# First block of a two-block transformer step: the recurrence's outputs with exchanged operands, and transfers inside SBUF in place of turns

## The reference, cut to what matters

```python
bu = einsum('bsgh,gph->bsgp', u, b_bar)          # 32 groups, 16 inputs, 64 complex states each
states = associative_scan(a_r * a_l, a_r * b_l + b_r) over the tokens
y = einsum('bsgp,ghp->bsgh', states, c_mat).real + d_skip * u
y = gelu(y.reshape(bsz, seq, 512))
y = y * sigmoid(y @ w_glu + b_glu)
mixed = concat([rmsnorm(y), rmsnorm(chunked_attention(q, k, v, rel_bias))])
```

## Time and profile before

| | us |
|---|---|
| median of 3 executions | 2977.44 (2976.95 to 2977.65) |
| span of the profiled execution, first to last instruction | 2975.0 |
| TensorE busy, of the span | 2961.7 |
| VectorE busy | 2261.4 |
| ScalarE busy | 1467.9 |
| the stage of the change | about 120 to 180 |

### The profile page before, as it was taken

How to read it: one execution, slowest core, us unless ns; L and a number is a source line. 1 busy time by engine, 2 the same in 40 slices (tenths; PEclk the granted TensorE clock), 3 DMA queues, 4 the chain that set the end, 5 groups by cost and what they waited for, 6 DMA issues and landing times.

```text
span 2975.0 us, 48001 instructions
## 1 busy us (share of the span) xinstructions
PE 2961.7 (100%) x18781; PEld 2655.5 (89%) x18781; DVE 2261.4 (76%) x2787; ACT 1467.9 (49%) x2155; POOL 58.1 (2%) x148
## 2 busy tenths in 40 slices
PE   9999999999999999999999999999999999999999
PEld 8779999888889999878899998888999878899998
DVE  7978888576759887566598875658888567588984
ACT  4476555454345555444455553325555354355554
POOL 6100000000000000000000000000000000000000
PEclk9999999999999999999999999999999999999999
DMA  6122332342133332311333333223333222133322
GB/s 189 49 72 92 101 125 93 111 137 71 56 101 99 99 105 100 94 64 56 105 101 99 99 107 105 87 68 115 102 100 106 92 85 66 62 114 99 106 99 78
DMA packets 256759, 283.30 MB, mean 95 GB/s; under 512 B 11938, under 2 KB 229216, under 8 KB 256616
## 3 DMA queue, kind: packets, MB, share of 16 engines
q1 hardware_dynamic: 256504, 281.28, 29.1%
q10 hardware_dynamic: 112, 0.02, 0.0%
HBM read 279.16 MB, written 4.73 MB: 95 GB/s over the span
## 4 chain that ended last, share of the span: by engine, by line
PE 89%; DVE 6%; ACT 2%; issue 1%; POOL 1%; DMA 1%; DVEq 0%; SPq 0%; ACTq 0%; POOLq 0%
PE ps L2946 39%; PE ps L2571 13%; PE ps L2573 13%; PE ps L2572 13%; PE ps L3303 1%; PE ps L3304 1%; PE ps L3305 1%; PE ps L3210 1%; PE ps L3270 1%; PE ps L3249 1%; PE ps L3289 1%; PE ps L3291 1%; PE ps L3290 1%; PE ps L3159 1%; PE ps L3140 0%
## 5 line engine op out<-in xcount | busy, mean ns | idle before, releaser
L840 ACT ACTIVATE whi<-raw 128x2048 fp32r<-128x2048 f32 (+2 forms) x144 | 246.6, 1712 | 467.8 <-PE ps L2573 386.7
L1519 DVE TENSOR_TENSOR wlo<-raw,whi 128x2048 fp32r<-128x2048 f32 (+2 forms) x144 | 293.6, 2039 | 219.5 <-ACT whi L840 219.2
L2946 PE MATMUL ps<-th,wh 128*128 128x256 f32 x1600 | 453.7, 284 | 0.6 <-DVE wl L1608 0.5
L2946 PE MATMUL ps<-tl,wh 128*128 128x256 f32 x1600 | 452.7, 283 | 0.0
L2946 PE MATMUL ps<-th,wl 128*128 128x256 f32 x1600 | 452.7, 283 | 0.0
L2571 PE MATMUL ps<-hh,whi 128*128 128x512 f32 x896 | 357.4, 399 | 0.0
L2573 PE MATMUL ps<-hh,wlo 128*128 128x512 f32 x896 | 349.7, 390 | 0.0
L2572 PE MATMUL ps<-hl,whi 128*128 128x512 f32 x896 | 349.4, 390 | 0.0
L2946 PE MATMUL ps<-hh,wh 128*128 128x256 f32 x1200 | 340.1, 283 | 0.2
L2946 PE MATMUL ps<-hh,wl 128*128 128x256 f32 x1200 | 339.6, 283 | 0.0
L2946 PE MATMUL ps<-hl,wh 128*128 128x256 f32 x1200 | 339.6, 283 | 0.0
(11 more groups left out here) (524 smaller groups left out, 6693.1 us busy)
## 6 DMA issues: line engine op xcount, KB each, us to landing
raw<-in_w_ffn_in SPq DMA_DIRECT2D x88, 1024.0 KB, 5.1
raw<-in_w_in SPq DMA_DIRECT2D x59, 1024.0 KB, 5.2
raw<-in_w_ffn_out SPq DMA_DIRECT2D x40, 1024.0 KB, 5.0
raw<-in_w_o SPq DMA_DIRECT2D x32, 640.0 KB, 4.0
raw<-in_w_gate SPq DMA_DIRECT2D x11, 1024.0 KB, 5.3
raw<-in_w_up SPq DMA_DIRECT2D x11, 1024.0 KB, 5.3
raw<-in_w_down SPq DMA_DIRECT2D x10, 1024.0 KB, 5.0
raw<-in_w_out SPq DMA_DIRECT2D x4, 1024.0 KB, 5.3
```

Source lines behind the costliest of these rows:

```text
L840: a.activation(whi[:, slot, 0:n], raw[:, slot, 0:n], ACT.Copy).then_inc(hi_made, 1)
L1519: v.tensor_tensor(wlo[:, u % 2, 0:n], raw[:, u % 2, 0:n], whi[:, u % 2, 0:n].bitcast(F32), ALU.subtract).then_inc(lo_made, 1)
L2946: e = mm(bank(b, HALF), wgt[:, q, w], xx, start=start and k == 0 and m == 0, stop=k == KD // 2 - 1 and m == 2, skip_group_check=True)
```

## The change

In `outputs(n)` the two operands of every matmul change places, so that bank 6 has phase and feature of one tile in its partitions (32 t + r) and the 128 token groups in its columns, tile by tile. `steps_out(n)` on ScalarE copies the bank to `ystep` as it is. The turns and the second copies are gone. SP moves the rows: for each n sixteen transfers, one for each phase and tile, each of 32 partitions with 128 values, from partition 32 t to partition 32 j of `yg`. They all count up `yg_loaded`, 256 for each n. SP issues portion 0 after bias(4), portion 1 after bias(6), portions 2 and 3 after bias(7), ahead of the last three units of output weights. `steps_out(n)` waits until the portion before has landed, since `ystep` is one buffer; `outputs(n)` waits for the copy of the portion before, and `gelu(c)` for the landing of portion c.

```diff
-        ytok = at("ytok", A0 + 61440, [P, 4, P])
+        ystep = at("ystep", A0 + 61440, [P, 4, NC])
@@ SyncE
             out1_unit(0)
+            def steps_to_features(n):
+                sp.wait_ge(S("steps_taken"), n + 1)
+                for t in range(4):
+                    for j in range(4):
+                        sp.dma_start(yg[32 * j:32 * j + 32, n, NC * t:NC * t + NC], ystep[32 * t:32 * t + 32, j, :]).then_inc(S("yg_loaded"), 16)
             for h in range(2, NH1):
                 bias(h)
+                if h in (4, 6):
+                    steps_to_features(h // 2 - 2)
+            steps_to_features(2)
+            steps_to_features(3)
             for j in range(1, 4):
                 out1_unit(j)
@@ ScalarE
             def gelu(c):
-                act.wait_ge(S("yg_ready"), c + 1)
+                act.wait_ge(S("yg_loaded"), 256 * (c + 1))
@@
-            def tokens_out(n):
+            def steps_out(n):
                 act.wait_ge(S("ssm_y"), n + 1)
                 if n:
-                    act.wait_ge(S("ssm_ytr"), n)
-                src = bank(6).rearrange("p (i t r) -> p t i r", i=4, t=4)
-                a.activation(ytok[:, :, :].rearrange("p t (i r) -> p t i r", i=4), src, ACT.Copy).then_inc(S("ytok_ready"), 1)
-
-            def features_out(n):
-                act.wait_ge(S("ssm_ytr"), n + 1)
-                a.activation(yg[:, n, :], bank(6 if n else 7), ACT.Copy).then_inc(S("yg_ready"), 1)
+                    act.wait_ge(S("yg_loaded"), 256 * n)
+                a.activation(ystep[:, :, :].rearrange("p i c -> p (i c)"), bank(6), ACT.Copy).then_inc(S("steps_taken"), 1)
@@ the loop over t on ScalarE
-                if t in (3, 5):
-                    features_out((t - 1) // 2)
-                if t == 2:
-                    features_out(0)
-                    tokens_out(t // 2)
+                    steps_out(t // 2)
-                    tokens_out(0)
+                    steps_out(0)
-                    tokens_out(1)
+                    steps_out(1)
@@ after gelu(0) on ScalarE
-            features_out(3)
@@ TensorE, outputs(n)
-                if n >= 2:
-                    pe.wait_ge(S("yg_ready"), n)
+                if n:
+                    pe.wait_ge(S("steps_taken"), n)
@@
-                    i, dst = 4 * n + j, bank(6, P, P * j)
-                    mm(dst, ut[:, i, :], tm[:, i, :], start=True, stop=False, skip_group_check=True)
+                    i, dst = 4 * n + j, bank(6, NC, NC * j)
+                    mm(dst, tm[:, i, :], ut[:, i, :], start=True, stop=False, skip_group_check=True)
                     for r in range(2):
-                        e = mm(dst, st[r][:, n % 2, j, :], cl[:, i, r, 1:5, :, :].rearrange("p s g h -> p (s g h)"), start=False, stop=r == 1,
+                        e = mm(dst, cl[:, i, r, 1:5, :, :].rearrange("p s g h -> p (s g h)"), st[r][:, n % 2, j, :], start=False, stop=r == 1,
                                skip_group_check=True)
@@ TensorE
-            def outputs_turned(n):
-                pe.wait_ge(S("ytok_ready"), n + 1)
-                if n == 0:
-                    pe.wait_ge(S("ssm_t"), 14 * 3 + 2)
-                for t in range(4):
-                    e = tr(bank(6 if n else 7, NC, NC * t), ytok[:, t, :], ident[:, :])
-                e.then_inc(S("ssm_ytr"), 1)
@@ TensorE, values(0) and the list of calls
-                    pe.wait_ge(S("yg_ready"), 1)
-            pe.wait_ge(S("ytok_ready"), 1)
+            pe.wait_ge(S("steps_taken"), 1)
-            outputs_turned(0)
-            outputs_turned(1)
-            outputs_turned(2)
-            outputs_turned(3)
@@ TensorE, gated product
-                        pe.wait_ge(S("yg_ready"), 4)
+                        pe.wait_ge(S("steps_taken"), 4)
```

More of the change, by code:

```diff
@@ L2818, in values @@
                     pe.wait_ge(S("ya_ready"), f)
-                else:
-                    pe.wait_ge(S("yg_ready"), 1)
                 for j in range(4):
```

## The result

The changed kernel takes 2986.22 us (median of 6, 2984.48 to 2987.58), the kernel before 2977.05 in the same measurement (2976.75 to 2977.65): ratio 1.0031, interval 1.0021 to 1.0041, or 9.2 us slower. The forecast was 2976.3, the range 2975.0 to 2982.0. The profile is that of the execution that took 2985.27 us.

A forecast was written before the change was run, and what follows sets the result against it. TensorE was taken as busy practically throughout, and the edited stage as bound by the chain through a ring of engines. Terms -0.95 - 0.44 - 0.34 + 0.64 = -1.09 us on 2977.44 gave 2976.3; range 2975.0 to 2982.0.

The forecast's parts named there:

- What bounds the stage, and what the removal gives: Stage from 120 to 180 us: chain through a ring of engines; removed turns and copies give at most 1.73 us.
- The operands exchanged, no cost: In outputs(n): twelve matmuls and weight loads of the same size as before, same 128x512 copy; no cost, no gain.
- the price of an issue: On SP's queue: each of 64 transfers takes 0.41 us to issue, taken from gain vectors at 0.36 to 0.46.
- The upper row: SP's bias transfers of 64 and 128 rows, up to 0.62 us apart when queued: far upper end for an issue.
- Landing, 2.4 us: A 16 KB transfer lands 2.4 us after issue, at worst 3.5, so sixteen free ystep after 8.55 us.
- the prediction's estimate of 33 us: Time for a group of sixteen transfers if they followed one another in full at about 2.0 us fixed cost each.
- How the price works on the end: Beyond 0.46 us an issue, three groups run in series: every 0.1 us costs 4.5 us, +7.7 at 0.62.
- hidden by 4 us: Fourth group of transfers: landed by 177.5 us, while the last GELU, which alone needs it, ran at 182.59.
- three signs of being wrong: In the profile after: ScalarE copy waiting beyond 147 us, VectorE waiting for a late bias transfer, stage clock under 1.00.
- Rival (c): SP's issuing becomes the bound, from 0.58 us an issue; 2985 us at 0.62, 2991 at 0.75; 8 in 100.
- Rival (e): TensorE's clock falls in the gap the first turns leave, 138 to 142 us; 2981 or above 2983.4; 2 in 100.
- Rival (d): Sixteen transfers run one after the other, 2.4 us each, 38.4 us a group; +90 us, 3067; 1 in 100.

The follow-up runs named there:

- the 26 turns without and with GpSimd: Changed kernel plus 26 identity transposes ahead of scores(5): 2985.80 us; the same with GpSimd issuing portions 1 and 3: 2981.23 us.
- the first set of probes: Changed kernel with each portion moved whole, rows left in place, then sixteen probe transfers within SBUF of varied rows, bytes and partitions: 2987.56 us in one execution.

## Why the prediction was wrong, step by step

**What bounds the stage, and what the removal gives: right.** -1.73 us was forecast with all additions hidden; the kernel with one transfer a portion measured -1.7, and that through device memory with the gap filled -1.5. The steps hold too. The profile of the kernel with one transfer is 0.33 us ahead of that before already at values(0) (146.20 against 146.53). Less this, its copy into ptb for 150.02 is 1.0 us earlier (0.95 forecast), turned(5) for 165.05 is 1.4 (1.39), and the copy for 173.23 is 1.9 (1.73). That the medians agree to 0.1 us is finer than their spread allows.

**The operands exchanged, no cost: right**, 0.0.

**The step that failed: the price of an issue**, "0.41 us, because the shape is that of the gain vectors". It is 0.63, and 0.66 over the first run of sixteen with its one long issue. Within SBUF the shape of rows and bytes, by which I chose the row, does not matter; what matters is that the gain vectors come from device memory and these transfers have SBUF at both ends. Even for device memory 0.41 was on the low side: in a run of sixteen such issues it is 0.46. The upper row, queued bias transfers 0.62 apart, was the right number by luck rather than by kind: they too read device memory.

**Landing, 2.4 us: nearly right.** The three landings that freed the buffer took 1.76, 2.93 and 1.75 us, 0.8 less in all than three times 2.4. The fixed cost of about 2.0 us, from which the prediction's estimate of 33 us comes, stands in the Trainium skill, DMA: Bandwidth & Descriptors, section Anatomy of one DMA, for transfers issued from GpSimd. The median from issue to landing is 2.0 us from GpSimd's queue here and 1.8 from SP's.

**How the price works on the end: right.** Three groups in series, each released by the one before; 45 intervals. (That SP is the bound from 0.58 on is the working's; no run puts all the groups at a price near it.) The text put 0.62 at +7.7 us. The 45 intervals measured 9.93, 9.45 and 9.42 us for each fifteen, 28.8 in all instead of 27.9; with 0.8 less for the landings that makes +7.8, and the profiled execution is 8.0 us longer by its span. The copy behind the first group came at 147.38 instead of 144.28, that behind the second at 165.89 instead of 158.33, that behind the third at 177.77 instead of 168.33. The fourth, "hidden by 4 us", was not: it landed at 190.94 and the last GELU began at 190.97, though that GELU was itself 8 us late, so that it cost about 0.1. With the copies freed it was the next bound, 3.3 us in the kernel with four buffers. Of the prediction's three signs of being wrong two came, ScalarE's copy waiting beyond 147 and a clock under 1.00; the third, VectorE waiting for a bias transfer, did not.

**Rival (c)** happened, and had been given 8 in 100. Its condition was worked out and its price was near; the chance was wrong, because no row had SBUF at both ends and I let the nearest shape stand for it. **Rival (e)**, the clock, happened too, in another place than forecast: in the gap of 3.4 us that SP's delay made. It happened in the forecast place as well, but not in every execution: the gap that the first turns leave is 1.35 to 1.36 us long in all ten profiles that have it, and behind it the clock stayed at 1.00 in six (the changed kernel's among them) and fell in four (four buffers, the 26 turns without and with GpSimd, and the first set of probes). Filling the second gap gave back nothing measurable in the changed kernel, and 5.2 us once part of SP's work was taken off it. **Rival (d)**, sixteen one after the other, did not: they left 0.63 us apart while each took 1.8 to land. The Trainium skill, DMA: Bandwidth & Descriptors, section Rules for kernel authors, says to coalesce transfers below 64 KB as mostly overhead. The runs agree, with the overhead on the issuing queue: sixteen of 16 KB held SP for 10.5 us, one of 256 KB for 0.6.

Open: the 1.2 us between the 8.0 of the profiled execution and the 9.2 of the medians lie within the spread of the executions, 2984.48 to 2987.58 us. That the spread of the versions in which SP is not the bound comes from the clock in the first gap is argued, not shown. For it speak the spans of the 11 executions with the gap filled, and four profiles: one of a shorter execution in each of the kernels with one transfer, through device memory and with the last portion whole (clock 1.00), and one of a longer execution with four buffers (0.74). But that one was late before the gap as well, and no kernel has a profile of both a shorter and a longer execution. Why an issue with SBUF at both ends is dearer for SP, no run shows.

## What to carry to other kernels

Price an issue from a row with the same memories at its two ends, rather than from one of the same size, and multiply it by the number in series before asking whether the bytes are hidden. A row whose source and destination differ in kind says little of another pair (here it was 0.17 us an issue short), and the range must then reach well past it. When a single small buffer is released by a transfer, the issuing queue sets the pace of whatever engine fills it; and work that looks superfluous on TensorE may be holding its clock, which one profile alone does not tell.

## What the runs showed of the hardware

An issue on SP's queue, sixteen in a row: 0.63 us from one to the next with SBUF at both ends, for 16 to 128 rows alike; 0.46 with device memory at either end, for 32 rows of 512 B. From GpSimd with SBUF at both ends: 0.50. Single issues vary more: the store of a portion to device memory was 0.58 us busy at the first and 0.34 at the last. A transfer of 16 KB within SBUF lands in 1.8 us by the median (1.7 to 3.1 in the changed kernel), one of 256 KB in 2.6 in the kernel with one transfer a portion. TensorE idle for 3.4 us was followed by a granted clock of 0.55 and 0.59 from 152 to 160 us while it was working again. Idle for 1.35 to 1.36 us, it kept the clock at 1.00 in six profiles, that of the changed kernel among them, and lost it in four (0.83 and 0.74 in two stretches behind it with four buffers); so such a gap does not decide alike each time.
